# Two transformer blocks on one core: the low part of the recurrent stage's split weights moves from VectorE to the pool engine

## The chip, the cores and the metric

The kernel runs on one core of a Trainium2 chip. The metric is the device time of one execution in microseconds (us). Before the change the median of three runs is 4316.08 us (4304.51 to 4337.88).

## The reference

The reference chains two small transformer stacks over 512 latent tokens and 256 context tokens, with 1024 features. The first has a layer with differential attention and a chunk MLP, and a layer with windowed attention with sinks, each followed by a SwiGLU network. The second has a gated linear recurrence in both directions (the part that the change touches), and a layer of latent attention.

The recurrent layer projects the 768 normalised tokens through a weight of 1024 by 5 x 2048. For each of 16 heads that gives q, the values, two forget gates (forward and backward) and an output gate z, each 128 wide. Its core, as the reference has it for one chunk:

```
b = jnp.cumsum(lfc, axis=1)
o_inter = jnp.einsum('bthk,bhkv->bthv', qc * jnp.exp(b), S)
decay = jnp.exp(jnp.where(tri, b[:, :, None] - b[:, None, :], -jnp.inf))
scores = jnp.einsum('bthk,btshk,bshk->bhts', qc, decay, kc)
o_intra = jnp.einsum('bhts,bshv->bthv', scores, vc)
```

The output of each head is normalised, multiplied by silu(z), and all heads go through an output projection.

## The kernel before

All tokens lie as features on the 128 partitions and tokens on the free axis: 768 columns (512 latent, 256 context). Weights stream from HBM in tiles of 128 x 1024 fp32 into ring buffers: ring B has 5 slots (`ringB`), ring A 4. SyncE issues the loads, one per slot, each behind a semaphore by which TensorE says that the slot was read.

**Split weights.** In some stages each fp32 product is made as three cheaper fp32r products. Weights W are split as high = round(W) and low = W - high, and the inputs likewise (`x_r` high, `a_r` low). `split_product` (L438 to L450) issues, for each of 8 blocks of 128 rows and for the two token ranges, high x `x_r`, high x `a_r` and low x `x_r`: 48 matmuls per tile. In the recurrent stage the high part goes to `ringA_r[:, s % 3]`, and the low part to `ringB_r[:, s]`. Five tiles per head (s = 0 q, 1 values, 2 and 3 gates, 4 z) and 16 heads make 80 tiles. In the four earlier stages that split weights the pool engine makes both parts (`split`, L394 to L400).

**Who makes the two parts in the recurrent stage.** ScalarE makes the high part (`high(h, s)`, L1253 to L1257, and for the first three tiles L1403 to L1406) as soon as the weight has landed and the high slot is free, and counts `hg_high`. VectorE makes the low part (`low(h, s)`, L1658 to L1661): it waits for `hg_high`, subtracts, and counts `splitB`, on which TensorE waits before the tile's first product (L461).

**One head.** While head h runs its recurrence, the projections of head h+1 are interleaved into TensorE's program by hand (`step`, L746 to L824). In TensorE's order: diagonal products (L753), tile 1 of the next head, `pairs(0)`, `pairs(1)`, first half of tile 2, `pairs(2)`, second half of tile 2, transposes of the values (L730), `pairs(3)`, tile 3 in halves around `pairs(4)`, `pairs(5)`, tile 4 in halves around `pairs(6)`, transposes of the keys (L791), state updates (L800), output products (L805, L811), first half of tile 0 of head h+2, the sum of squares (L821), and the second half of it.

`pairs(i)` (L733 to L744, its matmuls on L742) is level i of a doubling scheme with 7 levels. VectorE feeds it: `level(i)` (L1679 to L1706) multiplies keys (L1692, two instructions) and queries (L1695, which releases `pairs(i)` by `hg_lvl`), and then updates two running products (L1701, L1705). `select(i)` (L1711) merges the result of a level from PSUM.

VectorE's order in a head (`step`, L1724 to L1780): the diagonal (L1729), then for levels 1 to 6 `level(i)`, `select(i-1)`, and behind levels 1 and 3 a `low` (tiles 3 and 4 of head h+1). After the levels: keys times products (L1740, which releases L791), queries times products (L1744), a `low` (tile 0 of head h+2), the states (L1757, L1760), two `low` (tiles 1 and 2 of h+2), the variance (L1767, waits for L821), the next head's `prepare` (L1717), the reciprocal (L1771), the next head's level 0 (L1694 to L1705), the gate (L1775, L1779).

ScalarE's order in a head (`step`, L1259 to L1286): evacuate q of the next head and `high` of tile 3; values and `high` of tile 4; gates, with `high` of tile 0 of head h+2; z, and `high` of tiles 1 and 2; two evacuations for the keys (L1281); a square (L1284) and a square root (L1286).

The pool engine has no instruction in the recurrent stage.

The engines' programs are fixed orders, written by hand; nothing is scheduled at run time apart from the semaphore waits.

Of the kernel before, what the change touches and what calls it, by code (L numbers as in the profile page):

```python
# [6 lines left out]
F32 = mybir.dt.float32  # L7
F32R = mybir.dt.float32r
U8 = mybir.dt.uint8
ALU = mybir.AluOpType  # L10
# [16 lines left out]
HEADS = 16  # L27
# [3 lines left out]
RA, RB, RC = 4, 5, 4  # L31
# [30 lines left out]
RH = 3  # L62
# [24 lines left out]
def build(nc, streamA, streamB, streamC, x_in, ctx2_in, smalls_in, consts_in, lvl_in, sgu_in, out):  # L87
    with ExitStack() as ctx:
# [5 lines left out]
        def sem(name):  # L94
            if name not in sems:
                sems[name] = ctx.enter_context(nc.semaphore(name))
            return sems[name]

        def both(name, shape):

            with nc.sbuf_tensor(name, shape, F32) as v:
                pass
            return v, sb(name + "_r", shape, F32R)
# [9 lines left out]
        ringA, ringA_r = both("ringA", [P, RA, D])  # L113
        ringB, ringB_r = both("ringB", [P, RB, D])
# [19 lines left out]
        def SM(name):  # L134
            return smalls[:, SMALL[name][0]:SMALL[name][1]]
# [21 lines left out]
        def one(ap, g, j):  # L157

            return ap[:, bass.ds(g, 1), j, :].rearrange("p a t -> p (a t)")
# [17 lines left out]
        def readB_after(name, g, k):  # L177
            return RB + START_B[name] + g * RB + k + 1

        def landedA_at(name, g, k):  # L180
            return 16 * ((START_A[name] + k) // RA + 1) + g * (16 * COUNT[name][1] // RA)
# [7 lines left out]
        def landedB_at(name, g):  # L189
            return 16 * (START_B[name] // RB + 1) + g * 16  # L190
# [86 lines left out]
        def state(d, i):  # L277
            at = (d * 5 + i) * P
            return sq[:].rearrange("p a t -> p (a t)")[:, at:at + P]
# [111 lines left out]
        @block.gpsimd  # L391
        def _(pool):

            def split(ring, ring_r, slot, high_r, high_slot, done):  # L394

                high = high_r[:, high_slot, :]
                nc.gpsimd.tensor_tensor(high, ring[:, slot, :], ones[:, 0:1].broadcast_to([P, D]), ALU.mult)  # L397
                pool.drain()  # L398
                nc.gpsimd.tensor_tensor(ring_r[:, slot, :], ring[:, slot, :], high.bitcast(F32), ALU.subtract) \  # L399
                    .then_inc(sem(done), 1)  # L400

            def split_A(name):
                with pool.Fori(0, COUNT[name][0]) as g:
                    for s in range(RA):

                        pool.wait_ge(landedA[s], landedA_at(name, g, s))
                        split(ringA, ringA_r, s, ringB_r, s, "splitA")

            def split_B(name):
                with pool.Fori(0, COUNT[name][0]) as g:  # L410
                    for s in range(RB):
                        pool.wait_ge(landedB[s], landedB_at(name, g))

                        pool.wait_ge(readB, readB_after(name, g, s - (RB - RH if s < RB - RH else RH)))
                        split(ringB, ringB_r, s, ringA_r, s % RH, "splitB")

            pool.wait_ge(sem("consts_in"), 16)
            split_B("even")
            split_A("ffn_in0")
            split_A("odd")  # L420
            split_A("ffn_in1")


        @block.tensor
# [993 lines left out]
        def _(dve):  # L1418
            TT, TS, STT = nc.vector.tensor_tensor, nc.vector.tensor_scalar, nc.vector.scalar_tensor_tensor

            def norm(n):
# [56 lines left out]
                if n in SPLIT:  # L1478
                    low(DC - 2)
                    low(DC - 1)  # L1480
# [174 lines left out]
                        if u < 15:  # L1655
                            maxima(u + 1)

            def low(h, s):  # L1658

                dve.wait_ge(sem("hg_high"), h * RB + s + 1)  # L1660
                TT(ringB_r[:, s, :], ringB[:, s, :], ringA_r[:, s % RH, :].bitcast(F32), ALU.subtract).then_inc(sem("splitB"), 1)  # L1661

            def hgrn():
                og_g = H["og"].rearrange("p (g e) t -> p g e t", e=2)
                G8 = HEADS // 4
# [42 lines left out]
                def select(i):  # L1708

                    at = 2048 + 1024 * (i % 2)  # L1710
                    nc.vector.copy_predicated(flat(H["A"]), lvl[:, i, :], psf[:, at:at + T]).then_inc(sem("hg_sel"), 1)  # L1711

                def prepare(g, e):

                    hd, B = g * 2 + e, HP[e]
                    dve.wait_ge(sem("hg_k"), hd * 2 + 2)
                    TT(H["kl"][:, 0, :], B["k"][:, 0, :], B["k"][:, 1, :], ALU.add).then_inc(sem("hg_ksum"), 1)  # L1717

                def begin(g, e):

                    dve.wait_ge(sem("hg_q"), g * 2 + e + 1)
                    level(g * 2 + e, e, 0)

                def step(g, e, store, follow, ahead=True):  # L1724

                    hd, B = g * 2 + e, HP[e]
                    nxt = hd + 1
                    dve.wait_ge(sem("hg_diag"), hd + 1)
                    TT(H["A"], psf[:, 2048:2048 + T].rearrange("p (n c) -> p n c", c=P),  # L1729
                       ident.unsqueeze(1).broadcast_to([P, NT, P]), ALU.mult).then_inc(sem("hg_init"), 1)  # L1730
                    for i in range(1, LEVELS):
                        level(hd, e, i)
                        select(i - 1)
                        if follow and i in (1, 3):
                            low(nxt, 3 + i // 2)
                    dve.drain()
                    dve.wait_ge(sem("hg_A"), (hd + 1) * LEVELS)

                    for d in range(2):
                        TT(H["kl"][:, 2 * d + 1, :], B["k"][:, 1 - d, :], H["S"][:, 1 - d, :], ALU.mult).then_inc(sem("hg_kS"), 1)  # L1740
                        if d == 0:
                            select(LEVELS - 1)
                    for d in range(2):
                        TT(H["kl"][:, 2 * d, :], B["q"], B["P"][:, 1 - d, :], ALU.mult)  # L1744
                    if follow and ahead:
                        low(nxt + 1, 0)
                    dve.drain()

                    for i in range(5):
                        for d in range(2):  # L1750
                            n = CHUNKS[d][i]
                            if i == 0:
                                dve.wait_ge(sem("hg_add"), hd * 2 + d + 1)
                            add = psf[:, (4 - 2 * d) * 512 + n * P:(4 - 2 * d) * 512 + (n + 1) * P]
                            at = n * P + (P - 1 if d == 0 else 0)
                            if i == 0:
                                nc.vector.tensor_copy(state(d, i), add).then_inc(sem(f"hg_state{d}"), 1)  # L1757
                            else:
                                dve.wait_ge(sem(f"hg_state{d}"), hd * 5 + i)
                                STT(state(d, i), state(d, i - 1), B["P"][:, 1 - d, at:at + 1], add, ALU.mult, ALU.add) \  # L1760
                                    .then_inc(sem(f"hg_state{d}"), 1)

                    if follow and ahead:
                        low(nxt + 1, 1)
                        low(nxt + 1, 2)
                    dve.wait_ge(sem("hg_ms"), hd + 1)
                    TS(rstd[:], psf[:, 2048:2048 + T], 1.0 / P, EPS, ALU.mult, ALU.add).then_inc(sem("hg_ms_out"), 1)  # L1767
                    if follow:
                        prepare(*follow)
                    dve.drain()  # L1770
                    nc.vector.reciprocal(rstd[:], rstd[:]).then_inc(sem("hg_inv"), 1)  # L1771
                    if follow:
                        begin(*follow)
                    dve.wait_ge(sem("hg_ro"), hd + 1)
                    STT(B["z"], B["z"], SM("o_norm"), rstd[:], ALU.mult, ALU.mult)  # L1775
                    dve.drain()
                    if store:
                        dve.wait_ge(sem("og_out"), 16 * (hd + 1))
                    TT(og_stage if store else one(og_g, g - G8, e), psf[:, 3072:3072 + T], B["z"], ALU.mult) \  # L1779
                        .then_inc(sem("hg_free"), 1)  # L1780
# [2 lines left out]
                dve.sem_inc(sem("hg_ms_out"), 1)  # L1783
                dve.sem_inc(sem("hg_free"), 1)
                dve.sem_inc(sem("og_out"), 16)
                low(0, 3)
                low(0, 4)
                prepare(0, 0)
                low(1, 0)
                begin(0, 0)  # L1790
                low(1, 1)
                low(1, 2)
                for lo, hi, store in ((0, G8, True), (G8, HEADS // 2 - 1, False)):
                    with dve.Fori(lo, hi) as g:
                        step(g, 0, store, (g, 1))
# [111 lines left out]
            residual("ffn_out1", MOD["g2", 1], LAT, 3, 4, 4)  # L1907
            ada_last(1)
            norm(4)
            for s in range(3):  # L1910
                low(0, s)
            norm(5)
            hgrn()
            for c in range(1, DC):
                add_square(6, c)
# [176 lines left out]
```

## Time and profile before

| | us |
|---|---|
| median of three runs | 4316.08 |
| lowest and highest run | 4304.51, 4337.88 |
| the profiled execution | 4306.82 |
| its span, first to last instruction | 4305.0 |
| TensorE busy | 3924.9 (91%) |
| VectorE busy | 1629.0 (38%) |
| ScalarE busy | 1069.3 (25%) |
| pool engine busy | 533.4 (12%) |

Busy shares are of the whole span. The recurrent stage lies between about 2145 and 3290 us; the mean granted TensorE clock over the span is 0.946 of full speed. In the timeline each row is one or several instructions of one engine at one line: start, duration (of the group, where there are several), names of output and inputs, their count, and in brackets the idle time before and what ended it. A timeline row of an instruction that a port or a wait inside its execution holds up shows a longer duration, not an idle time.

### The profile page before, as it was taken

The page shows a single profiled execution, that of the slowest core. Times are in us where ns is not written, and L with a number is a line of the kernel's source. Part 1 is how long each engine was busy: PE and PEld are TensorE (multiplying, and loading weights), DVE is VectorE, ACT ScalarE, POOL GpSimd, SP SyncE. Part 2 cuts the span into 40 slices and gives each one's busy share as a digit, 9 for nine tenths or more (in the row PEclk, how much of TensorE's full clock was granted, in tenths as well). Part 3 has the DMA queues.
Part 4 walks back from the last instruction along what each step waited for, and adds up shares of the span by engine and source line. Part 5 has one row for each costly group of instructions (what it writes and reads, how often), then busy time and mean ns, then how long its engine had stood idle before and what let it go on. Part 6 is the DMA issues. An engine that isn't in the chain of part 4 may idle for free.

```text
span 4305.0 us, 50920 instructions
## 1 busy us (share of the span) xinstructions
PE 3924.9 (91%) x19922; PEld 2728.3 (63%) x19922; DVE 1629.0 (38%) x2554; ACT 1069.3 (25%) x1559; POOL 533.4 (12%) x252
## 2 busy tenths in 40 slices
PE   7888999999999998989999999999986978999988
PEld 4666588875566665765488888888874543444443
DVE  4544300000233332000147878878774032222211
ACT  4333111100122221111033333333330013333320
POOL 2220144410111103661000000000000000000000
PEclk9888999999988899999989999999997989999999
DMA  5121233331100013333211111111111100000001
GB/s 220 64 84 72 109 110 110 111 121 67 60 16 14 19 54 142 141 141 137 83 59 39 52 48 44 48 40 44 36 45 68 50 30 30 29 29 24 29 27 66
DMA packets 81437, 291.87 MB, mean 68 GB/s; under 512 B 8225, under 2 KB 10273, under 8 KB 80417
## 3 DMA queue, kind: packets, MB, share of 16 engines
q1 hardware_dynamic: 75632, 274.30, 18.2%
q10 hardware_dynamic: 5680, 15.73, 0.9%
q8 instruction: 101, 1.65, 0.2%
q14 instruction: 24, 0.19, 0.0%
HBM read 275.32 MB, written 14.68 MB: 67 GB/s over the span
## 4 chain that ended last, share of the span: by engine, by line
PE 41%; issue 35%; DVE 7%; POOLq 6%; POOL 5%; DVEq 3%; ACT 2%; DMA 1%; ACTq 0%; SPq 0%
PE ps L433 13%; PE ps L448 11%; POOLq L398 5%; POOL ringA_r L399 4%; PE ps L934 3%; PE ps L932 2%; PE ps L966 2%; DVEq L1696 2%; PE ps L742 1%; PE ps L800 1%; DVE rstd L1771 1%; DVE arena L1695 1%; PE ps L479 1%; PE ps L811 1%; PE ps L943 1%
## 5 line engine op out<-in xcount | busy, mean ns | idle before, releaser
L448 PE MATMUL ps<-x_r,ringB_r 128*128 128x512 f32 (+1 forms) x2848 | 994.9, 349 | 46.4 <-POOL ringA_r L399 28.9
L448 PE MATMUL ps<-x_r,ringA_r 128*128 128x512 f32 (+1 forms) x2848 | 1006.4, 353 | 18.5 <-ACT arena L1250 13.1
L433 PE MATMUL ps<-arena,ringA 128*128 128x512 f32 (+1 forms) x2208 | 797.6, 524 | 22.7 <-DVEq L1800 9.4
L433 PEld LDWEIGHTS ps<-arena,ringA 128*128 128x128 f32 x2208 | 421.6, 191 | 398.2 <-issue 378.9
L448 PEld LDWEIGHTS ps<-x_r,ringB_r 128*128 128x128 f32 x2848 | 540.9, 190 | 136.7 <-POOL ringA_r L399 33.5
L448 PEld LDWEIGHTS ps<-x_r,ringA_r 128*128 128x128 f32 x2848 | 541.2, 190 | 106.8 <-issue 27.2
L448 PE MATMUL ps<-a_r,ringA_r 128*128 128x512 f32 x1600 | 542.6, 339 | 0.0
L448 PE MATMUL ps<-a_r,ringB_r 128*128 128x512 f32 x1248 | 449.9, 361 | 0.0
L397 POOL TENSOR_TENSOR ringB_r<-ringA,consts 128x1024 fp32r<-128x1024 f32 x104 | 198.1, 1905 | 1161.2 <-DMA ringA<-streamA 1161.2
L448 PEld LDWEIGHTS ps<-a_r,ringA_r 128*128 128x128 f32 x1600 | 303.0, 189 | 34.7 <-issue 1.0
L1528 DVE TENSOR_TENSOR arena<-arena,ps 128x768 f32 (+1 forms) x44 | 36.2, 822 | 664.6 <-ACT arena L1112 383.2
L448 PEld LDWEIGHTS ps<-a_r,ringB_r 128*128 128x128 f32 x1248 | 239.1, 192 | 33.3
L399 POOL TENSOR_TENSOR ringA_r<-ringA,ringB_r 128x1024 fp32r<-128x1024 f32 x104 | 249.3, 2397 | 14.8
L1507 DVE SCALAR_TENSOR_TENSOR x<-ps,mod,x 128x512 f32<-128x512 f32 (+1 forms) x48 | 30.3, 660 | 484.0 <-PE ps L433 484.0
L1833 DVE TENSOR_REDUCE st<-ps 128x1 f32<-128x768 f32 x64 | 61.3, 958 | 291.4 <-PE ps L934 291.4
L742 PE MATMUL ps<-arena 128*64 128x64 f32 (+1 forms) x2496 | 116.9, 236 | 47.6 <-DVE arena L1695 36.5
L1053 ACT ACTIVATE sq<-x 128x768 f32<-128x768 f32 (+1 forms) x51 | 39.8, 784 | 459.4 <-DVE x L1507 430.2
L1518 DVE TENSOR_TENSOR rstd<-rstd,sq 128x768 f32<-128x768 f32 (+1 forms) x49 | 43.3, 884 | 289.2 <-ACT sq L1053 286.0
L433 PE MATMUL ps<-a,ringA 128*128 128x512 f32 (+3 forms) x320 | 136.5, 581 | 15.4 <-DVE arena L1816 15.4
L1036 ACT ACT_TABLE_LOAD x26 | 33.4, 1283 | 441.9 <-PE ps L503 441.9
L742 PEld LDWEIGHTS ps<-arena 128*64 128x64 f32 (+1 forms) x2496 | 102.2, 147 | 62.8 <-DVE arena L1695 42.6
L1343 ACT ACTIVATE arena<-ps,st 128x768 f32<-128x768 f32 x64 | 57.7, 902 | 281.0 <-DVE st L1835 281.0
(247 smaller groups left out, 4826.3 us busy)
## 6 DMA issues: line engine op xcount, KB each, us to landing
ringA<-streamA SPq DMA_DIRECT2D x236, 512.0 KB, 3.5
arena<-streamC SPq DMA_DIRECT2D x136, 512.0 KB, 5.6
ringB<-streamB SPq DMA_DIRECT2D x100, 512.0 KB, 3.5
x<-x_in SPq DMA_DIRECT2D x2, 3072.0 KB, 11.7
x_scratch<-x ACTq DMA_DIRECT2D x6, 1024.0 KB, 5.6
a<-streamC SPq DMA_DIRECT2D x8, 512.0 KB, 11.5
x<-x_scratch SPq DMA_DIRECT2D x2, 2048.0 KB, 8.6
x_scratch<-x ACTq DMA_DIRECT2D x2, 1536.0 KB, 8.7
```

Source lines behind the costliest of these rows:

```text
L397: nc.gpsimd.tensor_tensor(high, ring[:, slot, :], ones[:, 0:1].broadcast_to([P, D]), ALU.mult)
L398: pool.drain()
L399: nc.gpsimd.tensor_tensor(ring_r[:, slot, :], ring[:, slot, :], high.bitcast(F32), ALU.subtract) \
L433: mm = nc.tensor.matmul(ps[0:m, bank + half, 0:tn], ring[:, slot, w0 + k * P:w0 + k * P + m], src[:, k0 + k, t0:t0 + tn], start=start and ...
L448: mm = nc.tensor.matmul(ps[:, bank + half, 0:tn], wk, src[:, k, t], start=k == 0 and i == 0, stop=k == DC - 1 and i == 2)
L742: mm = nc.tensor.matmul(psf[r[0]:r[1], at:at + r[1] - r[0]], H["kl"][:, 2 + p, t], H["ql"][:, p, t], start=True, stop=True)
L932: nc.tensor.matmul(ps[:, b + half, 0:tn], B["qn"][:, u * P:(u + 1) * P], B["kn"][:, t0:t0 + tn], start=True, stop=False)
L934: mm = nc.tensor.matmul(ps[:, b + half, 0:tn], B["qp"][0:HEAD, u * P:(u + 1) * P], M["kpe"][0:HEAD, t0:t0 + tn], start=False, stop=True)
L966: mm = nc.tensor.matmul(ps[:, 6, :], B["v"][:, n, :], M["pT"][:, n, :], start=n == 0, stop=n == NT - 1)
L1343: nc.scalar.activation(M["p"][:, c, :], psf[:, 1024 * c:1024 * c + T], ACT.Exp, bias=st[:, 8 + c:9 + c], scale=MLA_SCALE, accum_out=st[:, ...
L1696: dve.drain()
L1833: nc.vector.reduce_max(st[:, c:c + 1], psf[:, 1024 * c:1024 * c + T], AX_X)
```

## The change

VectorE's `low(h, s)` and its calls are removed: three ahead of `norm(5)`, five before the first head, five in each `step`. The pool engine gets a loop over the heads, behind its last split of ring A, with the same subtraction of the same operands into the same slot, in the order s = 0 to 4, each behind the same semaphore `hg_high` and counting the same `splitB`. ScalarE's `high`, TensorE's and SyncE's programs are as before.

```diff
@@ block.gpsimd
             split_A("ffn_in1")
+
+            def low(h):
+
+                for s in range(RB):
+                    pool.wait_ge(sem("hg_high"), h * RB + s + 1)
+                    nc.gpsimd.tensor_tensor(ringB_r[:, s, :], ringB[:, s, :], ringA_r[:, s % RH, :].bitcast(F32), ALU.subtract) \
+                        .then_inc(sem("splitB"), 1)
+
+            with pool.Fori(0, HEADS) as h:
+                low(h)
@@ block.vector
-            def low(h, s):
-
-                dve.wait_ge(sem("hg_high"), h * RB + s + 1)
-                TT(ringB_r[:, s, :], ringB[:, s, :], ringA_r[:, s % RH, :].bitcast(F32), ALU.subtract).then_inc(sem("splitB"), 1)
...
                         select(i - 1)
-                        if follow and i in (1, 3):
-                            low(nxt, 3 + i // 2)
...
-                    if follow and ahead:
-                        low(nxt + 1, 0)
                     dve.drain()
...
-                    if follow and ahead:
-                        low(nxt + 1, 1)
-                        low(nxt + 1, 2)
                     dve.wait_ge(sem("hg_ms"), hd + 1)
...
-                low(0, 3)
-                low(0, 4)
                 prepare(0, 0)
-                low(1, 0)
                 begin(0, 0)
-                low(1, 1)
-                low(1, 2)
...
             norm(4)
-            for s in range(3):
-                low(0, s)
             norm(5)
```

## Rows read from the trace of the kernel before

**Rows 1.** Busy time by engine in one stretch: PE, PEld, DVE, ACT, POOL, clock, DMA.

```profile
2300.00:2600.00 300.00, 277.98 (x2215) 243.53 (x2214) 248.85 (x312) 102.22 (x112) 0.00 (x0) 0.99 0.15 48
```

**Rows 2.** Waits in 2300 to 3100 us: total us, times, longest.

```profile
PE ps L800 <- ACT arena L1281: 26.2, 12, 2.2
PE ps L742 <- DVE arena L1695: 15.9, 21, 0.9
```

**Rows 3.** The removed line L1661 over the kernel: min/median/max ns.

```profile
L1661 DVE TENSOR_TENSOR ringB_r<-ringB,ringA_r x80: 1201/1218/1229, 2153.8 to 3191.1; 128x1024 fp32r<-128x1024 f32 x80
```

**Rows 4.** Timeline of TensorE in one head: start, us, line, idle before.

```profile
2517.43 0.92 PE L742 MATMUL ps<-arena 128*64 128x64 f32 x24 [0.89 <-DVE arena L1695]
...
2539.92 1.50 PE L742 MATMUL ps<-arena 128*128 128x128 f32 x12
2545.46 1.47 PE L791 MATMUL ps<-consts,arena 128*128 128x128 f32 x12
```

**Rows 5.** Timeline of VectorE in the same head, first row one head earlier.

```profile
2442.98 0.96 DVE L1695 TENSOR_TENSOR arena<-arena 128x768 f32<-128x768 f32 x1
...
2506.39 1.02 DVE L1775 SCALAR_TENSOR_TENSOR arena<-arena,smalls,rstd 128x768 f32<-128x768 f32 x1
2507.56 0.96 DVE L1779 TENSOR_TENSOR ringA<-ps,arena 128x768 f32<-128x768 f32 x1 [0.15 <-issue]
...
2509.30 1.02 DVE L1692 TENSOR_TENSOR arena<-arena 128x384 f32<-128x384 f32 x2
...
2511.28 0.96 DVE L1701 TENSOR_TENSOR arena<-arena 128x768 f32<-128x768 f32 x1
2512.40 0.96 DVE L1705 TENSOR_TENSOR arena<-arena 128x768 f32<-128x768 f32 x1 [0.16 <-PE ps L742]
...
2514.36 1.22 DVE L1661 TENSOR_TENSOR ringB_r<-ringB,ringA_r 128x1024 fp32r<-128x1024 f32 x1
2515.48 1.02 DVE L1692 TENSOR_TENSOR arena<-arena 128x384 f32<-128x384 f32 x2
...
2537.70 0.95 DVE L1695 TENSOR_TENSOR arena<-arena 128x768 f32<-128x768 f32 x1
...
2542.07 0.96 DVE L1740 TENSOR_TENSOR arena<-arena 128x768 f32<-128x768 f32 x1 [0.17 <-issue]
...
2543.86 0.94 DVE L1740 TENSOR_TENSOR arena<-arena 128x768 f32<-128x768 f32 x1
...
2550.76 0.29 DVE L1757 COPY sq<-ps 128x128 f32<-128x128 f32 x1 [3.08 <-PE ps L800]
```

**Rows 6.** Timeline of ScalarE in the same head, first row one head earlier.

```profile
2442.90 1.05 ACT L1257 ACTIVATE ringA_r<-ringB 128x1024 fp32r<-128x1024 f32 x1
...
2505.39 1.05 ACT L1257 ACTIVATE ringA_r<-ringB 128x1024 fp32r<-128x1024 f32 x1
...
2510.96 1.05 ACT L1257 ACTIVATE ringA_r<-ringB 128x1024 fp32r<-128x1024 f32 x1
...
2536.27 1.06 ACT L1257 ACTIVATE ringA_r<-ringB 128x1024 fp32r<-128x1024 f32 x1
...
2546.37 1.99 ACT L1257 ACTIVATE ringA_r<-ringB 128x1024 fp32r<-128x1024 f32 x2
```

**Rows 7.** Timeline of the pool engine in the first stage.

```profile
46.45 2.35 POOL L399 TENSOR_TENSOR ringB_r<-ringB,ringA_r 128x1024 fp32r<-128x1024 f32 x1
...
78.31 2.66 POOL L399 TENSOR_TENSOR ringB_r<-ringB,ringA_r 128x1024 fp32r<-128x1024 f32 x1
...
109.46 2.35 POOL L399 TENSOR_TENSOR ringB_r<-ringB,ringA_r 128x1024 fp32r<-128x1024 f32 x1
```

**Rows 8.** Timeline of VectorE in the first stage, last row ahead of the recurrent stage.

```profile
46.43 3.24 DVE L1463 SCALAR_TENSOR_TENSOR a<-x,coef,ps 128x512 f32<-128x512 f32 x6
...
76.94 1.78 DVE L1540 TENSOR_TENSOR arena<-arena,consts 128x512 f32<-128x512 f32 x1
...
99.63 0.16 DVE L1564 TENSOR_TENSOR st<-st,esm 128x1 f32<-128x1 f32 x1
...
109.67 2.16 DVE L1564 TENSOR_TENSOR st<-st,esm 128x1 f32<-128x1 f32 x1
...
2175.68 3.24 DVE L1463 SCALAR_TENSOR_TENSOR a<-x,coef,ps 128x512 f32<-128x512 f32 x6 [3.00 <-PE ps L484]
```

## The prediction

> **What bounds the kernel now.** I read the busy time by stretch first. In 300 us in the middle of the recurrent stage TensorE is busy 278 us and VectorE 249 us, at a granted clock of 0.99, and the pool engine has nothing [rows 1]. TensorE looks like the bound, but VectorE is close behind, so the second view is who waits for whom: over 800 us, which hold 12 heads, TensorE stood 15.9 us in 21 waits for `hg_lvl`, the query products of L1695, and 26.2 us for ScalarE's key evacuation [rows 2]. The third view is the timeline of one head, which says where on VectorE's chain such a wait begins. From the gate product L1775 at 2506.39 to level 2 VectorE has no rest, and TensorE stands idle 0.89 us in front of `pairs(2)` at 2517.43, until L1695 of that level is done [rows 4, 5]. So from the sum of squares of one head to level 2 of the next VectorE sets the time. From there on TensorE sets it: L1695 of level 6 ends at 2538.65 and `pairs(6)` begins at 2539.92, 1.27 us later; the first key product L1740 ends at 2543.03 and L791 begins at 2545.46 [rows 4, 5]. At the end of the head VectorE idles 3.08 us in front of L1757 [rows 5].
>
> **What is removed.** 80 instructions of 1.22 us, 97 us of VectorE [rows 3]. Only those on the chain count. Of the five of a head, the one for tile 3 (2514.36 to the next start at 2515.48) stands ahead of level 2, on the chain: minus 1.12 us. The one for tile 4 stands behind level 3, where TensorE leads; those for tiles 0, 1 and 2 lie beside VectorE's idle time at the end of the head [rows 5]. They give nothing directly, but the slack of levels 4 to 6 grows by the 1.12 us of tile 4. And of the 1.12 us on the chain TensorE could take only the 0.89 us that it idles, if nothing came in their place.
>
> **What is added, and its price.** 80 subtractions on the pool engine. Its same instruction, same tile shape, takes 2.35 us in the first stage [rows 7], so 188 us over a stage of some 1100: the engine itself has ample time. What matters is what it does to VectorE. Look at the two one-element operations L1564: normally 0.16 us, but 2.16 us where it started at 109.67, beside a pool instruction that runs from 109.46 to 111.81 [rows 7, 8]. VectorE was held until the pool engine's end. In the other direction: L1540 ran until 78.72 and the pool instruction of 78.31 ended at 80.97 instead of 80.66. So the pool engine gets in behind the VectorE instruction in flight, and ends about 2.25 us after that one's end. Not every VectorE instruction is held: six L1463, with one input from SBUF and one from PSUM, take 3.24 us beside the pool instruction of 46.45 and 3.24 us at 2175.68 with an idle pool engine [rows 7, 8]. So I take: a VectorE instruction with two tensor inputs from SBUF is held until the pool instruction ends, one with a PSUM input is not.
>
> **Walking one head.** The pool engine starts when ScalarE has made the high part, and ScalarE's times are not moved by the edit [rows 6].
> - Tile 3: high part done at 2506.44. L1775 (two inputs from SBUF) started at 2506.39, 0.05 us earlier, and ends at 2507.41, so the pool engine waits for it and ends at about 2509.65. L1779 and the diagonal L1729 read PSUM and pass. L1692 at 2509.30 is held until then; with about 0.1 us of an instruction's start overlapping, plus 0.2 us [rows 5].
> - Tile 4: high part done at 2512.01. VectorE is in L1701 (2511.28, now 2511.5 to 2512.45), then the pool engine holds until 2514.70, and L1705, due at 2512.60, is held: plus 2.0 us [rows 5].
> - Tile 0 of the head after: high part done at 2537.33. VectorE is then in L1695 of level 6, now 1.12 us earlier against TensorE (2536.6 to 2537.5), which gets through; L1701 is held 2.2 us. Net against TensorE plus 1.1 us: the two L1740 then end at 2544.1 and 2545.9, while L791 begins at 2545.46 and needs the second only halfway, after six transposes (at about 2546.2) [rows 4, 5]. I cost it at nothing; its cover is 0.3 us wide, and if that is gone it costs up to 1.1 us per head.
> - Tiles 1 and 2: high parts from 2546.37 to 2548.36, the pool engine is busy until about 2552.2, where VectorE mostly idles and then reads PSUM (L1757, and L1760 with one state and PSUM) [rows 5, 6]. Nothing is paid. No row shows a COPY from PSUM beside the pool engine. Bounds: 0, and 1.4 us (from 2550.76 to 2552.2); I take 0, since L1463 is the nearest row. The Trainium skill (SBUF — State Buffer, the rules on which instructions share VectorE's second port pair with the pool engine) states a rule for both cases: the pair is locked for a whole instruction, and the second to issue is fully blocked; but a VectorE instruction with at most one SBUF input, outside its two-port modes, never contends. The trace agrees where it shows the case, with 2.16 against 0.16 us and 3.24 against 3.24 us [rows 8]; L1757, which no row shows, would by the rule cost nothing, and the sum would stay as it is, where the upper bound would make it 14 x 1.4 = 20 us more.
>
> Chain per head: 0.2 + 2.0 - 1.12 = plus 1.1 us. Every second head is a little different: there the tile-4 high part is done at 2443.95, inside L1695 of level 1 (2442.98 to 2443.94, now 0.2 us later), so L1701 is the one that is held, again by about 2.1 us [rows 5, 6]: the same sum. The low parts are done long before TensorE wants them: tile 3 at 2509.7, wanted behind `pairs(3)` at about 2525; tile 4 at 2514.7, wanted behind `pairs(5)`.
>
> In head 0 TensorE is behind, with tiles of its own to catch up, and hides it; head 15 has no splits under way. That leaves 14 heads: 14 x 1.1 = 15 us. The three low parts ahead of the stage lie beside VectorE's waits for the sum of squares, and the five before the first head beside its waits for projections: nothing. SyncE's loads wait for TensorE's reads alone and shift with it.
>
> **The sum.** The profiled execution took 4306.82 us, so it would be 4322; the median of the runs shown was 9.3 us above that execution, and against it the forecast is 4316.1 + 15 = 4331 us.
>
> **Rivals.**
> - *Pool engine first (slower).* The tile-3 race is won by 0.05 us, by ScalarE's end against L1775's start. If the pool engine holds the pair first, L1775 is held from 2506.39 until about 2508.85, plus 2.35 us; tile 4's instruction then lands in L1692 of level 1 and holds 2.2 us more. 4.55 - 1.12 = 3.4 us per head, 48 us in all: 4364 us. From 3.1 us per head this passes 1%. For it speaks how thin the margin is; against it, that both chains begin at the same event (the reciprocal L1771 ends), so that they don't drift, and that the pool engine needs a semaphore's time on top.
> - *No hold (faster).* Were the pool engine's work invisible to VectorE, the wait of 0.89 us before `pairs(2)` would go: 14 x 0.89 = 12 us, 4304 us. For it: the edit takes 97 us from an engine that is 83% busy here. Against it: 2.16 us against 0.16 [rows 8].
> - *More holds than I count.* Level 6's cover fails (1.1 us) or L1757 is held (1.4 us), or both: 1.1 + 1.1 to 1.1 + 2.5 us per head, 31 to 50 us, 4347 to 4366 us.
>
> **Chances.** Forecast 0.60; pool engine first 0.12; more holds 0.16; no hold 0.10; the edit does nothing measurable for another reason 0.02. The range runs from the no-hold end (4304) to the dear end (4364). About 1%, 43 us, is what a measurement of this kernel can tell from no change. No faster case reaches it, so faster has only 0.03, for what I overlook; slower takes pool-first and the dear half of more holds: 0.17; the rest, 0.80, is the same.
>
> **What would show it.** In the profile after, L1661 is gone and the pool engine shows 80 more subtractions, of 2.35 us to 3.3 us (the longer ones waited). VectorE's L1705 or L1701 of level 1 shows 3.1 us instead of 0.96 in each head, and L1701 of level 6 as well. TensorE's wait in front of `pairs(2)` grows from 0.9 to about 2.0 us. L1775 stays at 1.02 us: if it shows 3.3 us, the pool engine was first. If L1757 shows 1.7 us, PSUM reads are held too. A head would take about 1.1 us longer. If L1705 and L1701 keep 0.96 us, the hold is wrong and the kernel is faster.

## The result, and the profile after

The changed kernel takes 4334.85 us (median of 20 runs, 4319.02 to 4363.36) against 4311.84 us for the kernel before, run on the same chips (20 runs, 4297.66 to 4337.88). The ratio is 1.0052, with a 95% interval of 1.0032 to 1.0072: 22 us slower, 14 to 31 us. The forecast was 15 us slower, and "no change within 1%" the likeliest class. That 4331 us was forecast and 4334.85 us measured is closer than the step itself was: the forecast started from the median of three runs, 4316.08 us, which lies 4.2 us above that of the twenty. The profiled execution took 4329.59 us, its span 4327.8 us, 22.8 us more than before.

The line numbers of the changed kernel are up to 10 higher: L1697, L1700, L1706 and L1710 are the level's lines (before L1692, L1695, L1701 and L1705), L1716 the select, L1773 the gate product, L1743 the key products, L1758 the copy of a state, L752 `pairs`, L801 and L810 the key transposes and state updates, L427 the new subtraction on the pool engine.

Busy time by engine in the same 300 us as in [rows 1]: PE, PEld, DVE, ACT, POOL, granted clock, DMA share, GB/s.

```profile
2300.00:2600.00 300.00, 272.93 (x2141) 239.68 (x2141) 233.62 (x280) 101.47 (x112) 56.82 (x22) 0.97 0.15 48
```

VectorE is busy 233.6 us instead of 248.9. The 22 subtractions of 1.22 us that moved to the pool engine are 27 us, so at least 12 us have come back as longer records of what stayed (at least, because the same 300 us now hold 4.4 heads instead of 4.5). TensorE does less work in the same time (272.9 us busy against 278.0), at a clock of 0.97 against 0.99.

Waits between engines, 2300 to 3100 us: total us, times, longest. They answer to [rows 2].

```profile
PE ps L752 <- DVE arena L1700: 29.3, 22, 1.9
PE ps L810 <- ACT arena L1291: 26.2, 12, 2.2
```

TensorE's wait for VectorE's query products has gone from 15.9 to 29.3 us; the other is the same to the tenth. So what became dearer in TensorE's waits did so ahead of `pairs`.

VectorE's timeline in one head of the changed kernel, with the rows that answer to [rows 5]; the first row is from the head before it.

```profile
2446.65 3.05 DVE L1706 TENSOR_TENSOR arena<-arena 128x768 f32<-128x768 f32 x1
...
2509.89 1.02 DVE L1773 SCALAR_TENSOR_TENSOR arena<-arena,smalls,rstd 128x768 f32<-128x768 f32 x1
...
2512.80 1.27 DVE L1697 TENSOR_TENSOR arena<-arena 128x384 f32<-128x384 f32 x2
...
2515.02 0.96 DVE L1706 TENSOR_TENSOR arena<-arena 128x768 f32<-128x768 f32 x1
2516.14 3.01 DVE L1710 TENSOR_TENSOR arena<-arena 128x768 f32<-128x768 f32 x1 [0.15 <-PE ps L752]
...
2542.23 3.06 DVE L1706 TENSOR_TENSOR arena<-arena 128x768 f32<-128x768 f32 x1
...
2555.70 0.29 DVE L1758 COPY sq<-ps 128x128 f32<-128x128 f32 x1 [3.57 <-PE ps L810]
```

The pool engine's timeline in the same head: the tiles 3, 4, 0, and 1 with 2 in one row.

```profile
2510.01 3.16 POOL L427 TENSOR_TENSOR ringB_r<-ringB,ringA_r 128x1024 fp32r<-128x1024 f32 x1 [21.55 <-ACT ringA_r L1267]
2515.93 2.40 POOL L427 TENSOR_TENSOR ringB_r<-ringB,ringA_r 128x1024 fp32r<-128x1024 f32 x1 [2.76 <-ACT ringA_r L1267]
2542.06 2.41 POOL L427 TENSOR_TENSOR ringB_r<-ringB,ringA_r 128x1024 fp32r<-128x1024 f32 x1 [23.73 <-ACT ringA_r L1267]
2552.15 4.66 POOL L427 TENSOR_TENSOR ringB_r<-ringB,ringA_r 128x1024 fp32r<-128x1024 f32 x2 [7.68 <-ACT ringA_r L1267]
```

Read the two together. Tile 3's instruction starts at 2510.01, 0.12 us behind the gate product (0.12 or 0.13 us in each of the 14 heads), lasts 3.16 us instead of 2.35, since it waited, and ends at 2513.17; L1697 took 1.27 us instead of 1.02. Tile 4's ends at 2518.33; L1710, started at 2516.14, ends at 2519.15, so it ran its own 0.8 us only behind it. Tile 0's ends at 2544.47 and holds L1706 of level 6 for 2.1 us. The copy L1758 at 2555.70 lies inside the last pair (2552.15 to 2556.81) and takes 0.29 us, as ever.

TensorE in the same head, to be held against [rows 4]:

```profile
2522.08 0.92 PE L752 MATMUL ps<-arena 128*64 128x64 f32 x24 [1.79 <-DVE arena L1700]
...
2544.57 1.50 PE L752 MATMUL ps<-arena 128*128 128x128 f32 x12
2550.11 1.47 PE L801 MATMUL ps<-consts,arena 128*128 128x128 f32 x12
```

The wait in front of `pairs(2)` is 1.79 us instead of 0.89. From `pairs(6)` to the transposes it is 5.54 us in both kernels (5.54 in [rows 4]): the hold in level 6 is covered.

**A second view gives what the forecast lacked.** Cut the stage at the start of each head's state updates (L800, L810 after); each row is one head: its length, TensorE's busy time, the granted clock (then DMA share and GB/s). The kernel before, four consecutive heads:

```profile
2748.11:2815.43 67.32, 62.75 (x487) 0.97 0.15 46
2815.43:2881.23 65.80, 61.00 (x487) 1.00 0.13 41
2881.23:2948.57 67.34, 62.74 (x486) 0.97 0.12 40
2948.57:3014.36 65.79, 61.02 (x487) 1.00 0.13 41
```

The changed kernel, five heads:

```profile
2622.23:2692.41 70.18, 64.31 (x486) 0.95 0.14 44
2692.41:2760.90 68.49, 62.56 (x486) 0.98 0.14 45
2760.90:2829.27 68.37, 62.74 (x486) 0.98 0.15 46
2829.27:2897.77 68.50, 62.56 (x487) 0.98 0.12 39
2897.77:2964.59 66.82, 61.18 (x486) 1.00 0.13 41
```

A head at full clock went from 65.8 to 66.8 us, plus 1.0 us, where 1.1 was forecast. But each head can also hold a stretch at the lower of TensorE's two levels, worth 1.5 us. Before, 7 of the 14 heads cut in this way have it, every second one. After, 12 of 14 have it, and two of these twice: 14 stretches. They lie in two places. In the kernel before all 7, and in the changed kernel 8 of the 14, fall in the state updates, right behind the 2.18 us in which TensorE waits for ScalarE's key evacuation. Such a one is in the head that the rows above show; the updates take 4.46 us there (from 2553.77) and 2.94 us where the clock stays up:

```profile
2556.00:2558.00 2.00, 2.00 (x11) 0.50 0.00 0
```

0.50 is 1.2 of 2.4 GHz. The other 6 of the changed kernel begin within 1.5 us of the start of `pairs(2)`, behind the wait that the change made longer. The head that starts at 2692.41 has one; its state updates take 2.94 us:

```profile
2727.67 0.92 PE L752 MATMUL ps<-arena 128*64 128x64 f32 x24 [1.81 <-DVE arena L1700]
```

```profile
2730.00:2732.00 2.00, 2.00 (x8) 0.50 0.00 0
```

In the kernel before, the alternation goes with TensorE's waits. In every second head it waits 0.81 us in front of `pairs(1)` as well as 0.9 us in front of `pairs(2)`; in the others the first wait is at most 0.26 us. Of the first 13 heads seven have both waits, and the seven low stretches fall in the state updates right behind these seven. The row for `pairs(1)` of one of them:

```profile
2443.99 0.92 PE L742 MATMUL ps<-arena 128*64 128x64 f32 x24 [0.81 <-DVE arena L1695]
```

The 14 heads sum to 930.2 us before and 956.3 us after, plus 26.0 us. Of this 14 x 1.03 = 14.4 us is the longer head, and 11.6 us are left. Seven further stretches at the lower clock, of 1.5 us each, are 10.7 us of that. The rest of the two spans differs by 3 us the other way (2.3 us of it ahead of the stage, where the two kernels hardly differ).

### The profile page after: what moved, and what is told of

Read it like the earlier page. It is cut to its first block, busy times and chain, and to the rows that moved or that the text cites. A ratio compares the mean times of both kernels' runs of the same rounds, so it can differ in the third digit from the quotient of the medians.

```text
span 4327.8 us, 50977 instructions
## 1 busy us (share of the span) xinstructions
PE 3928.6 (91%) x19922; PEld 2734.5 (63%) x19922; DVE 1596.6 (37%) x2474; ACT 1069.3 (25%) x1559; POOL 737.4 (17%) x332
## 4 chain that ended last, share of the span: by engine, by line
PE 41%; issue 35%; DVE 7%; POOLq 5%; POOL 5%; DVEq 4%; ACT 2%; DMA 1%; ACTq 0%; SPq 0%
PE ps L443 13%; PE ps L458 11%; POOLq L398 5%; POOL ringA_r L399 4%; PE ps L944 2%; PE ps L942 2%; DVEq L1701 2%; PE ps L976 2%; PE ps L752 1%; PE ps L810 1%; DVE arena L1710 1%; DVE arena L1700 1%; PE ps L489 1%; PE ps L821 1%; POOL ringB_r L399 1%
## 5 line engine op out<-in xcount | busy, mean ns | idle before, releaser
L458 PE MATMUL ps<-x_r,ringA_r 128*128 128x512 f32 (+1 forms) x2848 | 1009.0, 354 | 18.5 <-ACT arena L1260 13.1
L443 PE MATMUL ps<-arena,ringA 128*128 128x512 f32 (+1 forms) x2208 | 796.7, 524 | 22.8 <-DVEq L1793 9.4
L427 POOL TENSOR_TENSOR ringB_r<-ringB,ringA_r 128x1024 fp32r<-128x1024 f32 x80 | 204.4, 2565 | 1028.3 <-ACT ringA_r L1267 851.3
L752 PE MATMUL ps<-arena 128*64 128x64 f32 (+1 forms) x2496 | 117.5, 236 | 62.7 <-DVE arena L1700 52.2
L752 PEld LDWEIGHTS ps<-arena 128*64 128x64 f32 (+1 forms) x2496 | 102.6, 148 | 78.0 <-DVE arena L1700 58.3
```

The costliest lines, as they stand in the source:

```text
L427: nc.gpsimd.tensor_tensor(ringB_r[:, s, :], ringB[:, s, :], ringA_r[:, s % RH, :].bitcast(F32), ALU.subtract) \
L443: mm = nc.tensor.matmul(ps[0:m, bank + half, 0:tn], ring[:, slot, w0 + k * P:w0 + k * P + m], src[:, k0 + k, t0:t0 + tn], start=start and ...
L458: mm = nc.tensor.matmul(ps[:, bank + half, 0:tn], wk, src[:, k, t], start=k == 0 and i == 0, stop=k == DC - 1 and i == 2)
L752: mm = nc.tensor.matmul(psf[r[0]:r[1], at:at + r[1] - r[0]], H["kl"][:, 2 + p, t], H["ql"][:, p, t], start=True, stop=True)
```

## The experiments

Seven kernels, in two groups, each with runs of the kernel before on the same chip. Heads and stretches are read from one profiled execution of each kernel, ratios from all its runs. Two questions: is the price of 1.0 us per head the hold on VectorE and decided by where it falls; and is it the pool engine's work or TensorE's longer idle that brings more of the lower clock?

**1. VectorE alone, made slower in the same place.**

```diff
-    TT(halves(H["ql"][:, p, :], h), halves(B["q"], h), P_queries, ALU.mult).then_inc(sem("hg_lvl"), 1)
+    for n_ in range(2 if i == 2 else 1):
+        if n_:
+            dve.drain()
+        last = TT(halves(H["ql"][:, p, :], h), halves(B["q"], h), P_queries, ALU.mult)
+    last.then_inc(sem("hg_lvl"), 1)
```

> The kernel before (low parts on VectorE, pool engine idle) with one VectorE instruction more per head on the chain: the query product of level 2 is made twice, which makes TensorE wait some 0.97 us longer (0.92 us and a short drain) in front of pairs(2). No pool work at all. Open question: with all low parts on the pool engine TensorE's clock was at its lower level for some 1.5 us in 12 of 14 heads instead of 7 of 14. Theory (the longer idle of TensorE in the head brings the clock drops, whatever causes the idle): heads at full clock last 66.8 us instead of 65.8, and clearly more than 7 of 14 heads show the 1.5 us of lower clock; in all 20 to 25 us slower than before. Rival (the pool engine's own work brings the drops): 66.8 us, but 7 of 14 heads with a drop as before, in all 13.6 us slower.

Ratio to before 1.0094 (1.0054 to 1.0133), 4358.39 us against 4315.39. Two consecutive heads of the profiled execution:

```profile
2449.51:2517.73 68.22, 62.45 (x487) 0.97 0.13 45
2517.73:2585.95 68.22, 62.57 (x487) 0.97 0.14 46
```

The state updates of its first two heads, in the chain of waits:

```profile
2314.45 2.94 PE ps L800 x24
2381.25 4.41 PE ps L800 x24
```

The one head that begins at the upper clock takes 66.80 us (2314.45 to 2381.25), as forecast; the 12 after it take 68.2 us or more. The last of the 14, which has no splits under way and is shorter, has a low stretch too, so 13 of 14 have one. As in the changed kernel they lie in the state updates (9) and behind `pairs(2)` (5). No pool instruction runs in this stage, so the pool engine's work is not what lowers the clock: a VectorE chain that is longer by the same amount does it too. The 14 heads take 954.7 us, 24.5 more than before, within the 20 to 25 of the forecast; in all it cost about 40 us. In its profiled execution the stage already begins 32 us later than in the kernel before (2314.45 against 2282.58), though all is alike ahead of it: between 900 and 1300 us its granted clock was 0.88 and not 0.95. The heads cost what the theory says; the total of this execution has that loss of an earlier stage in it, which I come back to below. Whether the other runs of this kernel have it, no trace shows.

**2. No subtraction anywhere.**

```diff
-    nc.gpsimd.tensor_tensor(ringB_r[:, s, :], ringB[:, s, :], ringA_r[:, s % RH, :].bitcast(F32), ALU.subtract) \
-        .then_inc(sem("splitB"), 1)
+    pool.sem_inc(sem("splitB"), 1)
...
-    (ring_r[:, slot, w], x_r))):
+    (high_r[:, high_slot, w] if hg else ring_r[:, slot, w], x_r))):
```

The kernel leaves out the low part of the recurrent stage's weights: the same matmuls run on other numbers.

> The changed kernel without any subtraction: the pool engine waits and counts, and TensorE's third product takes the high part again in place of the low part, so the low part of the recurrent stage's weights is left out of the result; everything else is as in the changed kernel. Theory (VectorE's chain sets the time only by the 0.89 us in front of pairs(2), and the rest of the change's cost is the hold on VectorE): a head at full clock lasts 64.9 us, against 65.8 before and 66.8 with the change; 12 us less than before over 14 heads, 1 to 2 us less per head than with the change. Rival (VectorE's freed 97 us all count): 5 x 1.2 us less per head, some 80 us less. Rival (the cost of the change is the late low parts and not a hold): VectorE's instructions of level 1 keep 3 us here too.

Ratio 0.9965 (0.9935 to 0.9994). Two heads of this kernel:

```profile
2472.79:2537.61 64.82, 61.11 (x487) 1.00 0.14 48
2537.61:2602.42 64.81, 60.94 (x487) 1.00 0.14 48
```

64.8 us, forecast 64.9, and each of its 14 heads at a clock of 1.00. VectorE's instructions of level 1 are back at 0.96 us:

```profile
2500.73 0.96 DVE L1705 TENSOR_TENSOR arena<-arena 128x768 f32<-128x768 f32 x1
2501.84 0.96 DVE L1709 TENSOR_TENSOR arena<-arena 128x768 f32<-128x768 f32 x1 [0.16 <-PE ps L751]
```

So the whole of VectorE's 97 us is worth only 1.0 us per head at full clock, and with the hold the change costs 2.0 us per head against what it could have given. The 14 heads take 905.6 us, 24.7 less than before and not 12, since the seven low stretches are gone with it.

**3. Tile 3 alone on the pool engine.**

```diff
+ON_POOL = (3,)
+ON_DVE = tuple(s for s in range(5) if s not in ON_POOL)
...
-    pe.wait_ge(sem("splitB"), splitB_after(name, g, s))
+    if name != "hg":
+        pe.wait_ge(sem("splitB"), splitB_after(name, g, s))
+    elif s in ON_POOL:
+        pe.wait_ge(sem("splitP"), g * len(ON_POOL) + ON_POOL.index(s) + 1)
+    else:
+        pe.wait_ge(sem("splitB"), START_B["hg"] + g * len(ON_DVE) + ON_DVE.index(s) + 1)
```

The pool engine's loop makes tile 3 alone and counts `splitP`, and VectorE's `low` leaves that tile out.

> Of the five low parts of a head only that of tile 3 is made by the pool engine (with a semaphore of its own); the other four stay on VectorE where they were. It is the one that stood on VectorE's chain, and its pool instruction starts behind the gate product, beside instructions that read PSUM. Theory: minus 1.12 us, plus 0.2 to 0.3 us of hold in L1692 of level 1; of that TensorE takes its idle time of 0.89 us, so a head at full clock lasts 64.9 to 65.0 us, 10 to 12 us less than before in all, ratio about 0.997. Rival (any pool instruction in the levels costs its 2.35 us): 65.8 - 1.1 + 2.3 = 67 us per head, 17 us more than before.

Ratio 0.9978 (0.9947 to 1.0009): the interval still holds 1. The heads are clear:

```profile
2344.76:2409.77 65.01, 61.13 (x487) 1.00 0.14 48
2409.77:2474.76 64.99, 60.95 (x486) 1.00 0.14 47
...
2799.72:2866.12 66.40, 62.38 (x486) 0.97 0.12 41
```

65.0 us at full clock, 0.8 us less than before. Four heads have a low stretch. Heads 1 to 8 have none, with the same waits in front of `pairs` as the four (at most 1.1 us). The 14 heads take 913.9 us, 16.3 us less than before.

**4. The pool engine first at the gate product.**

```diff
+    high(nxt, 3)
     evacuate(nxt, 0, 0, B["q"], ACT.Silu, "hg_q")
-    high(nxt, 3)
```

> The changed kernel with ScalarE's high part of tile 3 made ahead of the evacuation of q instead of behind it, 0.7 us earlier. The pool engine then asks for the port while VectorE is still in L1705 of level 0, and gets it ahead of the gate product L1775. Theory of the hold (who comes first keeps the other out for the whole instruction): the gate product shows about 3.1 us instead of 1.02, the 0.25 us in L1692 of level 1 goes, level 1 keeps its hold by tile 4; a head at full clock lasts 1.8 us longer than in the changed kernel, 68.6 us, and the kernel is some 25 us slower than the changed one, 45 to 50 us slower than before. Rival (the two share the port by turns, and the 3 us in level 1 have another cause, such as a late operand): no change against the changed kernel.

Ratio 1.0162 (1.0111 to 1.0212), some 70 us slower than the kernel before. The long records in VectorE's timeline of this kernel, three of one head and one of the next:

```profile
2551.13 3.01 DVE L1773 SCALAR_TENSOR_TENSOR arena<-arena,smalls,rstd 128x768 f32<-128x768 f32 x1
...
2558.00 2.94 DVE L1706 TENSOR_TENSOR arena<-arena 128x768 f32<-128x768 f32 x1
...
2585.14 3.05 DVE L1706 TENSOR_TENSOR arena<-arena 128x768 f32<-128x768 f32 x1
...
2618.68 2.26 DVE L1710 TENSOR_TENSOR arena<-arena 128x768 f32<-128x768 f32 x1
```

and two heads:

```profile
2383.81:2453.99 70.18, 62.82 (x486) 0.98 0.13 44
2453.99:2526.46 72.47, 65.16 (x487) 0.93 0.12 43
```

The gate product takes 3.01 us, as the rule of the hold wants it; in the head that follows, the pool engine was earlier still and held the running product of level 0 (2.26 us) instead, and so in turn through the stage. 70.18 us less one stretch of 1.5 us is 68.7, forecast 68.6. The other kind of head, 72.5 us, can't be reduced like this, since part of its low stretches lies ahead of `pairs(2)`, where VectorE sets the time. All 14 heads have a low stretch, 11 of them more than one. The heads take 993.5 us, 63.3 more than before, and the total is 20 to 25 us beyond the forecast. (Its profiled execution also has the loss between 900 and 1300 us.) With one instruction of ScalarE 0.7 us earlier the change costs three times as much.

**5. Tile 4 alone.** The edit is that of experiment 3 with `ON_POOL = (4,)`.

> Of the five low parts only that of tile 4 is made by the pool engine; its removal from VectorE gives nothing, as it stood behind level 3 where TensorE leads. Theory (the hold in level 1 is the whole price): L1705 or L1701 of level 1 shows 3.0 us, a head at full clock lasts 65.8 + 2.1 = 67.9 us, and since TensorE idles 3 us in front of pairs(2), most heads also show the 1.5 us of lower clock: 14 x 2.1 + some 10 = 40 us slower than before. Rival (the price of the change lies in the sum of all five holds, in equal parts): 67.9 would be out of reach, some 66.2 us per head.

Ratio 1.0104 (1.0073 to 1.0135). VectorE in level 1 of this kernel:

```profile
2521.92 2.97 DVE L1724 TENSOR_TENSOR arena<-arena 128x768 f32<-128x768 f32 x1 [0.16 <-PE ps L759]
```

and two heads:

```profile
2632.83:2701.93 69.10, 62.55 (x487) 0.98 0.14 45
2701.93:2772.80 70.87, 64.16 (x487) 0.95 0.13 43
```

Every head has the lower clock; taking one stretch (1.5 us) and two (3.1 us) off leaves 67.6 and 67.8, forecast 67.9. The 14 heads take 978.0 us, 47.8 more than before (40 forecast). With this one moved, the kernel is slower than with all five. Tile 3's subtraction, 1.12 us on VectorE's chain, stays here and is gone in the changed kernel, and the hold is the same.

**6. Tiles 0, 1 and 2.** The edit is that of experiment 3 with `ON_POOL = (0, 1, 2)`.

> The low parts of tiles 0, 1 and 2 are made by the pool engine, those of tiles 3 and 4 stay on VectorE. Theory: tiles 1 and 2 cost nothing, beside VectorE's idle time and its reads of PSUM; tile 0 holds the running product of level 6 by 2.1 us. In the changed kernel that was covered by the 1.12 us that tile 4 had left free; here this is missing, the second key product ends at 2547.0 on the clock of the kernel before, TensorE wants it at 2546.2: a head at full clock lasts 66.6 us, 0.8 us more than before. Rival (the cover is wide enough anyway): 65.8 us, no change. Rival (the copies from PSUM at the end of the head are held as well): 68 us and a copy L1757 of 1.7 us.

Ratio 1.0050 (1.0029 to 1.0071). The hold, and a copy from PSUM beside the pool engine, in VectorE's timeline of this kernel:

```profile
2548.70 3.15 DVE L1714 TENSOR_TENSOR arena<-arena 128x768 f32<-128x768 f32 x1
...
2563.86 0.29 DVE L1776 COPY sq<-ps 128x128 f32<-128x128 f32 x1 [4.10 <-PE ps L817]
```

and two heads:

```profile
2698.23:2766.70 68.47, 62.83 (x487) 0.98 0.13 45
2766.70:2833.58 66.88, 61.44 (x487) 1.00 0.15 47
```

66.9 us at full clock; 66.6 was forecast. Here tile 0's subtraction catches the query product of level 6 (L1714) itself and not the running product behind it, since VectorE has tile 4's subtraction to do and is 1.1 us later against TensorE than in the changed kernel. TensorE waits for it in front of `pairs(6)`:

```profile
2551.91 1.60 PE L759 MATMUL ps<-arena 128*128 128x128 f32 x12 [0.81 <-DVE arena L1714]
```

So it was right that the cover is missing here, and the place of the hold was one instruction off. The copy is not held. The low stretches, in 12 of 14 heads, all lie in the state updates.

**7. All five on the pool engine, two of them later.**

```diff
     pool.wait_ge(sem("hg_high"), h * RB + s + 1)
+    if timed and s == 4:
+        pool.wait_ge(sem("hg_lvl"), h * LEVELS - LEVELS + 4)
+    if timed and s == 0:
+        pool.wait_ge(sem("hg_kS"), h * 2 - 2)
...
-    with pool.Fori(0, HEADS) as h:
+    low(0, False)
+    low(1, False)
+    with pool.Fori(2, HEADS) as h:
```

> The changed kernel, all five low parts on the pool engine, but two of them start later: tile 4 waits in addition for the query product of level 3, tile 0 for the key products behind level 6. Their holds of 2.1 us then fall into levels 3 and 4, where VectorE has 0.95 + 1.12 us in hand, and into the queries' products at the end of the head, where it idles afterwards. Theory (the cost of the change is where the holds fall, not that they exist): a head at full clock lasts 65.0 us as with tile 3 alone on the pool engine, no or few heads show the lower clock, and the kernel is 12 to 18 us faster than before, ratio 0.996 to 0.997. Rival (each hold costs wherever it falls): 67 us per head or more, slower than before.

Ratio 0.9962 (0.9942 to 0.9982), 4295.38 us against 4313.41: 16 us faster than the kernel before by the ratio, and so faster than both the kernel before and the changed one. Against tile 3 alone (0.9978, 0.9947 to 1.0009) the intervals overlap. VectorE's holds, in its timeline of this kernel:

```profile
2524.20 3.17 DVE L1712 TENSOR_TENSOR arena<-arena 128x768 f32<-128x768 f32 x1
...
2547.52 3.99 DVE L1753 TENSOR_TENSOR arena<-arena 128x768 f32<-128x768 f32 x2
```

and two heads:

```profile
2812.85:2877.90 65.05, 60.95 (x486) 1.00 0.13 41
2877.90:2942.96 65.06, 61.11 (x487) 1.00 0.13 42
```

The holds are as long as ever, 2.2 and 2.1 us, but they lie in level 3 and in the queries' products at the head's end. A head takes 65.05 us, forecast 65.0.

## Why the prediction was right, and where its size was off

- *VectorE sets the time from the sum of squares to level 2, TensorE afterwards.* Shown: without any subtraction a head gains 1.0 us and no more (experiment 2), and 0.97 us more on that chain cost 1.0 us (experiment 1).
- *The hold.* Shown in both orders: 3.0 us for L1710 or L1706, and 3.01 us for the gate product once the pool engine comes first (experiment 4). The copy from PSUM, for which no row of before stood, keeps 0.29 us beside the pool engine. The Trainium skill (SBUF — State Buffer, Who interferes with whom) has the rule that a VectorE instruction with at most one SBUF input, outside its two-port modes, does not contend with the pool engine: the trace agrees, with 0.29 us beside it and 0.29 us in [rows 5].
- *Tile 3: plus 0.2.* It was 0.25 us. The race was won in all 14 heads: the gate product takes 1.02 us in each. The margin, from the gate product's start to the end of ScalarE's high part, is 0.04 us in the head shown. The prediction gave a reason that it wouldn't drift, and it didn't, but with so little in hand the win was also luck; experiment 4 shows the other side of it.
- *Tile 4: plus 2.0.* 3.01 - 0.96 = 2.05 us in the timeline; alone, 1.8 us per head (experiment 5).
- *Tile 0: nothing, with a cover of 0.3 us.* In the changed kernel 5.54 us from `pairs(6)` to the transposes as before; without tile 4's 1.12 us of slack it costs 1.1 us (experiment 6), 0.81 us of it as a wait in front of `pairs(6)`.
- *Tiles 1 and 2, and what lies ahead of the stage: nothing.* As forecast.
- *About 1% is what a measurement can tell from no change.* That was too wide: with 20 runs on either side, 0.5% stands clear of none (interval 1.0032 to 1.0072).
- *The sum.* 14 heads of 1.1 us forecast, 14 of 1.0 us measured. **The term that was missing** is TensorE's clock: 10.7 to 11.6 us of the 26.0 us that the stage grew. The prediction took the granted clock of 0.99 in [rows 1] as full clock and left it there. Cut by heads, it would have shown 1.00 and 0.97 in turn: each second head already lost 1.5 us. With one half of the heads losing it and the other not, a change in idle time was to be priced at up to 7 x 1.5 = 10.5 us more or less.

How this goes with TensorE's waits in front of `pairs` between 2300 and 3100 us, by kernel, one profiled execution each. The last column has the low stretches in the state updates and those that begin elsewhere, at or near `pairs(1)` or `pairs(2)`.

| kernel | wait in front of `pairs`, us | longest, us | a head at full clock, us | heads with a low stretch | in the updates, elsewhere |
|---|---|---|---|---|---|
| no subtraction | 6.4 | 0.8 | 64.8 | 0 of 14 | 0, 0 |
| all on the pool engine, timed | 7.6 | 1.1 | 65.05 | 1 of 14 | 1, 0 |
| tile 3 alone | 8.7 | 1.1 | 65.0 | 4 of 14 | 4, 0 |
| before | 15.9 | 0.9 | 65.8 | 7 of 14 | 7, 0 |
| tiles 0, 1, 2 | 27.5 | 1.2 | 66.9 | 12 of 14 | 12, 0 |
| VectorE alone, slower (experiment 1) | 27.0 | 2.3 | 66.8 | 13 of 14 | 9, 5 |
| changed kernel | 29.3 | 1.9 | 66.8 | 12 of 14 | 8, 6 |
| tile 4 alone | 39.6 | 3.0 | 67.6 | 14 of 14 | 5, 16 |
| pool engine first (experiment 4) | 40.6, with 13.1 for the diagonal | 3.0 | 68.7 | 14 of 14 | 10, 20 |

Broadly, the more TensorE waits in the levels, the more heads have a low stretch, with or without the pool engine at work. Low stretches outside the state updates come in the four kernels whose longest wait is 1.9 to 3.0 us, and in none of the five with 0.8 to 1.2 us. That a longer wait brings more of the lower clock, whatever causes it, is what experiment 1 shows, with no pool engine in it, and experiments 2 and 7 from the other side. The wait of one head doesn't settle it: in experiment 3 eight heads stay up and four later ones with the same waits don't. What in the idle time the chip reacts to stays open, and with one execution of each kernel a difference of a few heads may be chance.

**Still open.** In two of the profiled executions (experiments 1 and 4) the clock was 0.88 and 0.87 between 900 and 1300 us, against 0.95 in the kernel before, and the stage began some 30 us later, though those kernels have the same programs up to there. In experiment 7 it was 0.91, and the stage began 8 us later; that kernel has a single low stretch. In experiments 5 and 6 it was 0.96 and 0.94, with low stretches in 14 and 12 heads. So the clock between 900 and 1300 us doesn't decide how many heads of the recurrent stage have one. The runs of one kernel spread by 17 to 49 us. For the kernels of experiments 1 and 4 the total therefore says less than the heads.

## What to carry to other kernels

Moving elementwise work from VectorE to the pool engine need not free VectorE for as long as that work lasted. Here the VectorE instruction that met the pool engine's subtraction with two inputs from SBUF was held until the pool engine was through, and 1.2 us removed came back as 2.1 us. What counts is not how much is moved but where the pool instruction starts: look in the timeline for the stretches where VectorE reads PSUM, idles, or is ahead of its consumer, and make the pool engine wait for a semaphore that puts it there. Read what lost slack costs TensorE by the granted clock per iteration, not by its mean over many.

## What the runs showed of the hardware that I had not expected

- The pool engine gets in between two VectorE instructions that follow each other within 0.1 to 0.2 us, and a wait of its own lengthens its instruction's record: 3.16 us instead of 2.35.
- One of five moved subtractions alone (tile 4) made the kernel 1.0% slower, all five together 0.5%: moving tile 3's as well takes 1.12 us off the chain on which tile 4's hold falls.
- TensorE's lower level came in stretches that cost 1.5 us each, in 0 to 14 of 14 heads, for waits that differ by 2 to 3 us per head. They lay in the state updates, behind a wait of 2.18 us, and in the four kernels that waited up to 1.9 to 3.0 us in front of `pairs` also there.
